# Hybrid recurrent and neighbourhood-attention block: the exponential of attention unit 1 earlier in ScalarE's order, three pieces of work behind it later

## The reference

```
xr, kx, vx, gx, qx, mrx, mnx = split(modulate(x) @ w_in)      # the context has xr, kx, vx
y_rnn = h_x * gelu(gx)                                        # gated linear recurrence
s = concat([q_rot . k_rot + bias  (8 x 16 window), q . k_ctx])
y_na = softmax(s) @ concat([v, v_ctx])                        # 16 heads of 64
x = x + m2 * ((sigmoid(mrx) * (y_rnn @ w_rnn_out) + sigmoid(mnx) * (y_na @ w_na_out)) @ w_out)
x = x + m5 * conv_ffn(...)
```

## Time and profile before

| | |
|---|---|
| median of 3 runs | 2252.68 us (2252.66 to 2253.31) |
| profiled execution, its own time | 2253.74 us |
| its span | 2252.0 us |
| TensorE busy | 2137.7 us, 95% |
| VectorE busy | 1405.9 us, 62% |
| ScalarE busy | 955.6 us, 42% |
| mean granted TensorE clock | 0.988 |

### The profile page before, as it was taken

How to read it: one execution, slowest core, us unless ns; L and a number is a source line. 1 busy time by engine, 2 the same in 40 slices (tenths; PEclk the granted TensorE clock), 3 DMA queues, 4 the chain that set the end, 5 groups by cost and what they waited for, 6 DMA issues and landing times. The chain is left out here.

```text
span 2252.0 us, 29048 instructions
## 1 busy us (share of the span) xinstructions
PE 2137.7 (95%) x10958; PEld 1812.6 (80%) x10958; DVE 1405.9 (62%) x2572; ACT 955.6 (42%) x1472; POOL 268.6 (12%) x202
## 2 busy tenths in 40 slices
PE   5989999999999999999986999979999999999999
PEld 1878888888889888898875888857888888888887
DVE  6678597785977859768587446666553245424442
ACT  3556665666656666566566211013221122112220
POOL 0031222112221122121230000000000000000000
PEclk9999999999999999999999999989999999999999
DMA  8411212012120121201112644421121111111112
GB/s 310 120 46 38 68 40 76 29 38 68 38 78 29 38 69 38 78 21 46 50 56 79 235 153 150 146 84 62 65 84 47 47 47 47 56 56 47 47 54 96
DMA packets 68632, 167.56 MB, mean 74 GB/s; under 512 B 22704, under 2 KB 28208, under 8 KB 68400
## 3 DMA queue, kind: packets, MB, share of 16 engines
q1 hardware_dynamic: 47520, 145.20, 19.0%
q0 software_dynamic: 4608, 16.78, 2.1%
q10 hardware_dynamic: 16400, 4.19, 0.9%
HBM read 145.17 MB, written 25.17 MB: 76 GB/s over the span
## 5 line engine op out<-in xcount | busy, mean ns | idle before, releaser
L48 PE MATMUL t_o_ps<-qh,xnh 128*128 128x384 f32 (+1 forms) x640 | 223.3, 349 | 0.3 <-PEq L173 0.3
L49 PE MATMUL t_o_ps<-ql,xnh 128*128 128x384 f32 (+1 forms) x640 | 207.4, 324 | 0.0
L50 PE MATMUL t_o_ps<-qh,xnl 128*128 128x384 f32 (+1 forms) x640 | 207.4, 324 | 0.0
L1383 DVE TENSOR_TENSOR probT_low<-t_o_ps,probT_high 128x512 fp32r<-128x512 f32 (+2 forms) x256 | 138.9, 584 | 56.5 <-ACT probT_high L1086 55.3
L1843 ACT CAST wh<-raw 128x1024 fp32r<-128x1024 f32 x68 | 70.9, 1045 | 192.0 <-PE pd L50 170.1
L806 PE MATMUL f_ps<-xnh,wh 128*128 128x512 f32 x360 | 149.1, 414 | 2.4 <-ACT stage L1022 2.3
L1086 ACT CAST probT_high<-t_o_ps 128x512 fp32r<-128x512 f32 (+2 forms) x256 | 117.0, 510 | 59.5 <-PE t_o_ps L897 51.5
L808 PE MATMUL f_ps<-xnh,wl 128*128 128x512 f32 x360 | 142.0, 394 | 0.0
L807 PE MATMUL f_ps<-xnl,wh 128*128 128x512 f32 x360 | 142.0, 394 | 0.0
L48 PE MATMUL pg<-yh,wh 128*128 128x512 f32 x352 | 136.9, 389 | 0.0
L49 PE MATMUL pg<-yl,wh 128*128 128x512 f32 x352 | 136.9, 389 | 0.0
(11 more groups left out here) (311 smaller groups left out, 5620.4 us busy)
## 6 DMA issues: line engine op xcount, KB each, us to landing
raw<-w_ff SPq DMA_DIRECT2D x68, 512.0 KB, 3.2
raw<-w_fm SPq DMA_DIRECT2D x32, 512.0 KB, 6.6
raw<-w_qkv SPq DMA_DIRECT2D x24, 512.0 KB, 3.9
raw<-w_mix SPq DMA_DIRECT2D x24, 512.0 KB, 4.4
bias<-bias_d SPq DMA_DIRECT2D x16, 448.0 KB, 5.8
wm<-w_modk SPq DMA_DIRECT2D x8, 768.0 KB, 7.6
row_c<-w_modT SPq DMA_DIRECT2D x12, 512.0 KB, 3.3
raw<-w_modT SPq DMA_DIRECT2D x12, 512.0 KB, 3.3
```

The lines of the kernel that those rows point to most:

```text
L48: pe.matmul(out, w_hi(k), x_hi(k), start=(k == 0), stop=False)
L49: pe.matmul(out, w_hi(k), x_lo(k), start=False, stop=False)
L50: last = pe.matmul(out, w_lo(k), x_hi(k), start=False, stop=(k == chunks - 1))
L1383: dve.tensor_tensor(probT_blocks(ptl, u, bank), probT_bank(u, bank), probT_blocks(pth, u, bank).bitcast(F32), ALU.subtract).then_inc(pt_lo, 1)
```

## The change

Three things move; no instruction is added or taken out.

- ScalarE: `soft(i, 1)` and `probT_high(i, 0)` now stand directly behind the copies of jobs 4, 5 and 6. The high exchange of job 4 was inside these copies and now stands behind `probT_high(i, 0)`. Behind it come the Tanh of `F_MR+1` and then the cast of MN's weights (before: the cast, then the Tanh). `soft(i, 2)` follows `probT_high(i, 1)` as before.
- VectorE: `split_low(MN)` moves from ahead of unit 0 to the end of unit 1. In the last turn it stands elsewhere and does not move.
- TensorE: the two pieces of unit 1 are left out; one piece more stands in unit 4 and one more in unit 6, each between the scores and the weighted values.

```
                         prob_transposes(i, u)
-                        if not last and (u % 2 == 1 or u == ATT - 2):
+                        if not last and u >= 3 and (u % 2 == 1 or u == ATT - 2):
                             piece()
                         if u + 2 < ATT:
                             scores(i, u + 2)
-                        if not last and u % 2 == 1 and u < ATT - 1:
+                        if not last and (u in (4, 6) or u % 2 == 1 and 3 <= u < ATT - 1):
                             piece()
...
+                def exchange_high(i, n):
+                    dst, other, c0, cols, _ = TR_JOBS[n]
+                    act.wait_ge(tr_hi, i * JOBS + n + 1)
+                    for h, rows in enumerate(HEAD_ROWS):
+                        last = act.copy(other[HEAD_ROWS[1 - h], h, c0:c0 + cols],
+                                        dst[rows, h, c0:c0 + cols].bitcast(F32))
+                    last.then_inc(high_exchanged, 1)
...
-                        if other is not None:
-                            act.wait_ge(tr_hi, i * JOBS + n + 1)
-                            for h, rows in enumerate(HEAD_ROWS):
-                                last = act.copy(other[HEAD_ROWS[1 - h], h, c0:c0 + cols],
-                                                dst[rows, h, c0:c0 + cols].bitcast(F32))
-                            last.then_inc(high_exchanged, 1)
+                        if n in JOBS_A and other is not None:
+                            exchange_high(i, n)
...
                     soft(i, 0)
                     tr_high(i, JOBS_B)
+                    soft(i, 1)
+                    probT_high(i, 0)
+                    exchange_high(i, 4)
                     if last:
                         branch(i, LAST_MN + 1, 3, False, F_ps)
                     else:
+                        branch(i, F_MR + 1, 1, first)
                         split_hi(MN, raw_count(MN, i))
-                        branch(i, F_MR + 1, 1, first)
                     for u in range(ATT):
                         if u % 2 == 1 and u >= 3:
                             bottoms(i, (u - 3) // 2)
-                        probT_high(i, u)
-                        if u + 1 < ATT:
+                        if u > 0:
+                            probT_high(i, u)
+                        if 0 < u < ATT - 1:
                             soft(i, u + 1)
...
                     tr_low(i, JOBS_B)
-                    if not last:
-                        split_low(MN, i)
                     for u in range(ATT):
                         probT_low(i, u)
                         inverse(i, u)
...
+                        elif u == 1:
+                            split_low(MN, i)
                         elif u == 4:
                             split_low(G, i)
```

## The result

| | before | changed |
|---|---|---|
| median of 5 runs | 2253.31 us | 2263.87 us (2261.46 to 2265.37) |
| profiled execution, its span | 2253.74, 2252.0 | 2261.46, 2259.7 |
| mean granted clock of the span | 0.988 | 0.984 |

The changed kernel is slower: ratio 1.0046, 95% interval 1.0034 to 1.0057, +10.6 us in the medians, where +9.0 was forecast. The traced execution is the fastest of the five, +7.7 us.

What follows compares the result with a forecast made beforehand. TensorE, busy 95% of the span, was taken as the bound, so only its idle time and clock count. +2.0 us of moved waits and +7.0 of clock gave +9.0, 2261.7 us; range 2254.0 to 2266.5.

Steps and rivals of the forecast that it cites:

- The stall moves from unit 1 to unit 2 and loses its cover: TensorE ahead of unit 2's transposes: idle about 2.4 us as listed, waiting for unit 2's exponential, without the two pieces.
- ScalarE wins only 0.23: ScalarE ahead of unit 2's exponential: it starts at 323.20, before 323.43, since 2.84 us of work now stands ahead of it.
- +0.33 a turn: TensorE's balance per turn: unit 2's transposes -0.50, pieces in units 4 and 6 +0.53 and +0.30; bounds -0.3 and +0.9.
- Clock: five falls of seven at 1.4: TensorE's clock behind the new gap falls to the lower level in five turns of seven, 1.4 us each: +7.0 us.
- Eight waits, "the number of turns": TensorE ahead of the probability transposes: eight waits averaging 1.65 us, ending with unit 0's low parts, read as one per turn.
- MN's low parts are in time, by 0.3 us: VectorE's split of MN's weights, moved behind maxima(3), still in time for the first piece; thinnest cover, 0.3 us.
- The clock holds: Rival: the gap at unit 2 opens but at most one clock fall follows; +2.0 to +3.4 us, chance 0.20.
- The pieces are not hidden: Rival: pieces in units 4 and 6 delay the outputs; +6.0 us with steady clock, 2265.7 with the clock's part; chance 0.10.
- Faster: Rival: ScalarE reaches unit 2's exponential in time, saving 2.7 us a turn, 2234 us; chance 0.05.
- Nothing comes of it: Rival: unit 1's exponential is not what held its transposes and all shifts cancel; 2252.7 us, chance 0.03.

Runs made afterwards that it cites:

- e5: The changed kernel with ScalarE's cast of MN's weights moved behind the exponential of unit 2 and the Tanh of F_MR+1 behind that of unit 3; 2249.66 us, ratio 0.9980.
- e1: The changed kernel with ten added 512-column matmuls, result overwritten, behind scores(3) in the gap ahead of unit 2; 2256.18 us, ratio 1.0013.
- e2: The changed kernel with two added 512-column matmuls, result overwritten, behind scores(3) in the gap ahead of unit 2; 2263.86 us.
- e4: The kernel before with only ScalarE's order changed: exponential of unit 1 directly behind the job copies, then the exchange of job 4; 2270.26 us, ratio 1.0074.
- e3: The kernel before with TensorE's part alone: the two pieces of unit 1 moved to units 4 and 6; 2257.71 us, ratio 1.0018.
- e11: The changed kernel with four added 512-column matmuls, result overwritten, behind scores(3) in the gap ahead of unit 2; 2256.18 us.
- e12: The kernel of e7 run again unchanged: e5 with the last chunk of F_MR+1 held back behind scores(2); 2244.34 us, ratio 0.9963.
- e7: e5 with the last of the eight chunks of F_MR+1 held back from ahead of unit 0 to behind scores(2); 2246.14 us, ratio 0.9967.
- e9: e5 with the two extra pieces in units 12 and 14, not 4 and 6, and the Tanh of F_MN behind unit 10; 2246.46 us, ratio 0.9970.

## Why the prediction was right

- *The stall moves from unit 1 to unit 2 and loses its cover.* Right, and shown: 2.44 us listed on the exponential, forecast about 2.4; e5 removes it by ScalarE's order alone.
- *ScalarE wins only 0.23.* Before, the exponential of unit 2 started at 323.43; now at 322.94, of which 0.30 is the turn's earlier start, so 0.19.
- *+0.33 a turn.* Measured 142.15 - 141.82 = 0.33. The pieces in units 4 and 6 hide as forecast. Seven turns and the last one, +2.0 in the sum, came to +1.6 in the trace: 6 x 0.33 for the second to the seventh, -0.3 for the first with the start of the mixer, which I had counted as +0.33, and -0.1 for the last, which I had counted as -0.3. In the last turn the waits of units 1 and 2 were 1.15 and 0.96 before and are 0.64 and 1.47 now, so there the wait only moved. e1's median shows +2.8.
- *Clock: five falls of seven at 1.4.* In the trace four at 1.53 us, 6.1 in place of 7.0. In the medians 7.7 by e1. If each fall costs 1.53, that is five; this count was not read from the runs without a trace. That five was the right count is in part luck. Nothing in the rows gave the share of turns, and it does not simply follow the length of the gap: 1.97 us had five falls in its trace, 2.44 four, 2.79 six.
- *Eight waits, "the number of turns".* A misreading of the earlier trace rows: seven are unit 1's, 1.86 each, and the eighth is 0.21 in the last turn (1224.11). The sum used seven, so nothing came of it.
- *MN's low parts are in time, by 0.3 us.* Right: no wait stands at unit 3 or the first piece in the trace.
- *The rivals.* "The clock holds" is refuted by the low stretches of four turns and by e1. Gaps of 2.44 and even 1.97 us were followed by the lower level in four and five turns of seven. The Trainium skill's page "TensorE: Matmul & The Clock Gate", in its section on why this matters for kernels, asks only that there be no gaps above some 3 us; these traces do not agree. "The pieces are not hidden" is refuted by the rows at 332.66 and 339.78. "Faster" needed ScalarE in time; e5 shows that this does give a faster kernel. "Nothing comes of it" is refuted by the interval of the ratio.
- What I did not foresee: in this trace the falls come in a row, four turns running, while I thought of them as one chance for each turn. In e2 (second, third, fifth to seventh turn) and e4 (all but the fourth) they stand together less neatly; what picks the turns was not tried.

## What to carry to other kernels

Before moving an instruction out of a critical stretch, list what it is moved in front of: 2.84 us of ScalarE's work went from ahead of one exponential to ahead of the next, and the filler work was taken away from exactly there. Keep independent work where TensorE waits, and price a gap of about 2 us not by its length only but by what the clock does behind it: here 0.33 us of plain loss a turn came with 1.5 us more in four turns of seven. When a clock effect is suspected, put useless work in the gap: if the kernel gets faster, it is the clock.

## What the runs showed of the hardware

- *Which gaps the clock survives.* Idle times are as the traces list them. Before: 0.24 (1.66 in the first turn), 1.4 us of work, 1.86: no fall in seven turns. e3: 0.21, 1.86, then 1.4 us of work and 0.96: none. e11: 0.63, 1.4 us of work, 1.52 behind 0.9 us of added work: none. e2: 0.63, then 1.97: five. Changed: 0.63, then 2.44: four. e4: 2.79: six. So 1.97 fell where 1.86 did not; whether the 0.63 ahead of it has a part in that was not tried. The sum of two neighbouring gaps does not decide alone: 1.66 and 1.86 held in the first turn before, 0.63 and 1.97 fell. Longer gaps do not fall every time either.
- *A tiny VectorE instruction that takes 1.04 us.* The 128x1 minimum that ends the maxima took 0.16 in all eight units read before (310.8 to 338.6). In e12 VectorE and GpSimd read:
```profile
326.09 1.04 DVE L1391 TENSOR_TENSOR stat<-stat 128x1 f32<-128x1 f32 x1
```
```profile
326.07 1.04 POOL L752 TENSOR_TENSOR stage<-stage,half_one 128x512 f32<-128x512 f32 x1
```
GpSimd's multiply had begun 0.02 us before, and the minimum ends as it ends. ScalarE's exponential of unit 4 waits 0.57 for it, and that is the wait at unit 4 in e5 and e12, in each of the seven turns. In the kernel before, the same minimum took 0.35 later in the turn (348.95), under a GpSimd addition that ran from 348.24 to 349.28, and ended as that ended. In e7's trace the same two met the other way round:
```profile
324.07 0.16 DVE L1391 TENSOR_TENSOR stat<-stat 128x1 f32<-128x1 f32 x1
```
```profile
324.07 1.07 POOL L752 TENSOR_TENSOR stage<-stage,half_one 128x512 f32<-128x512 f32 x1
```
and the turn is 0.38 us shorter, in all seven turns. e9 has both cases in one trace. Six of its turns collide, as the fourth:
```profile
609.21 1.04 DVE L1387 TENSOR_TENSOR stat<-stat 128x1 f32<-128x1 f32 x1
```
The fifth does not:
```profile
750.10 0.16 DVE L1387 TENSOR_TENSOR stat<-stat 128x1 f32<-128x1 f32 x1
```
and it alone has no wait at unit 4 and takes 140.50 us in place of 140.90 (743.15 to 883.65). The Trainium skill's page "SBUF — State Buffer", in its section on the two sides of SBUF, says that the port pair shared by VectorE and GpSimd is an exclusive lock, that a VectorE instruction with two SBUF inputs takes it against a GpSimd instruction that reads SBUF, as the two here do, and that whoever starts first gets it for the whole instruction. The rows agree for VectorE: 1.04 against 0.16 for the same instruction, decided by some hundredths of a microsecond. On GpSimd's side they show little: 1.07 in place of 1.04. A VectorE reciprocal, which has one input, began inside such a multiply in the kernel before (1177.22, the multiply from 1176.91) and took its usual 0.15. The collision came about because e5 moved the Tanh of F_MR+1, and with it GpSimd's sigmoid, beside the maxima of unit 4. No run with the Tanh elsewhere was made, so the gain of a version without the collision (0.38 x 7 = 2.7 us by the two traces) is an estimate from them.
